# The last layer normalization of a decoder step: weight multiplied in by GpSimd, shift and bias as a rank-six product in PSUM, one pass of VectorE

## The reference

```python
def layer_norm(x, g, b):
    xf = x.astype(F32)
    mu = jnp.mean(xf, -1, keepdims=True)
    var = jnp.mean(jnp.square(xf - mu), -1, keepdims=True)
    return ((xf - mu) * lax.rsqrt(var + LN_EPS) * g.astype(F32) + b.astype(F32)).astype(x.dtype)
...
h = layer_norm(DN_ALPHA * x + mixed, ln1_g, ln1_b)
f, fbuf = conv_ffn(h, ffn_buf, ffn_w_up, ffn_conv_w, ffn_w_down)
y = layer_norm(DN_ALPHA * h + f, ln2_g, ln2_b)
```

## Time and profile before

| | us |
|---|---|
| median of 3 runs | 2952.71 |
| lowest, highest | 2946.45, 2958.77 |
| span of the profiled execution (first to last instruction) | 2947.1 |
| its own time | not given by the page |
| last chunk of the down projection | about 2824 to 2919 |
| tail, behind the last product | about 2919 to 2947.1 |

### The profile page before, as it was taken

One profiled execution on the slowest core, in us unless ns is written; L12 is line 12 of the kernel. 1 busy time (PEld: TensorE's weight loads), 2 busy tenths in 40 slices (PEclk: granted clock), 3 DMA queues, 4 the chain that ended last, 5 costly groups with the idle time before them and its releaser, 6 DMA issues.

```text
span 2947.1 us, 55566 instructions
## 1 busy us (share of the span) xinstructions
PE 2788.9 (95%) x22685; PEld 2676.0 (91%) x22685; DVE 2278.0 (77%) x3537; ACT 1384.8 (47%) x2371; POOL 359.2 (12%) x332
## 2 busy tenths in 40 slices
PE   8999999999989969999889999999999999999996
PEld 8999999988888658889889999999999999999996
DVE  6656877877657777755688888888888888878898
ACT  4434545545646544522264444444444453434344
POOL 0010000013370315223330000000000000000002
PEclk9999999999989989999999999999999999999998
DMA  7564444448722884563344444444343464434343
GB/s 221 179 206 107 117 119 128 113 150 286 275 82 105 343 247 117 148 175 92 90 157 136 119 126 117 137 115 132 111 141 111 137 194 163 153 112 155 114 124 118
DMA packets 521474, 440.14 MB, mean 149 GB/s; under 512 B 36264, under 2 KB 476767, under 8 KB 515147
## 3 DMA queue, kind: packets, MB, share of 16 engines
q1 hardware_dynamic: 456662, 300.70, 35.6%
q0 software_dynamic: 20288, 82.91, 7.6%
q10 hardware_dynamic: 44272, 52.98, 5.3%
HBM read 378.31 MB, written 66.55 MB: 151 GB/s over the span
## 4 chain that ended last, share of the span: by engine, by line
PE 49%; DVE 5%; issue 1%; ACT 1%; POOL 1%; DMA 1%; DVEq 0%; ACTq 0%; POOLq 0%
PE i L3363 42%; PE i L140 7%; DVE f_half L3869 1%; DMA x_blocks<-s_blk 1%; POOL x_blocks L3311 1%; DVE x_blocks L3907 1%; DVE h_rows L3902 0%; DVE y_rows L4000 0%; DVE w_ring L3858 0%; DVE x_blocks L3835 0%; PE i L3372 0%; DVE y_rows L3993 0%; DVE f_sum L3862 0%; DVE ln_parts L3913 0%; ACT x_blocks L3657 0%
## 5 line engine op out<-in xcount | busy, mean ns | idle before, releaser
L3363 PE MATMUL i<-x_blocks,f_half 128*128 128x272 f32 x10752 | 1357.0, 288 | 26.0 <-DVE h_rows L3902 10.9
L3363 PEld LDWEIGHTS i<-x_blocks,f_half 128*128 128x128 f32 x10752 | 1347.0, 189 | 31.7 <-DVE x_blocks L3907 14.1
L570 PE MATMUL a<-xb_in,w_half 128*128 128x272 f32 x4200 | 546.9, 291 | 8.9 <-DVE w_half L972 4.6
L570 PEld LDWEIGHTS a<-xb_in,w_half 128*128 128x128 f32 x4200 | 536.0, 190 | 18.2 <-issue 7.2
L3586 ACT CAST f_half<-w_ring 128x1024 fp32r<-128x1024 f32 (+2 forms) x370 | 346.2, 936 | 403.1 <-PE i L3363 339.5
L3869 DVE TENSOR_TENSOR f_half<-w_ring,f_half 128x1024 fp32r<-128x1024 f32 (+2 forms) x362 | 393.4, 1087 | 80.3 <-ACT f_half L3586 77.9
L3869 DVE TENSOR_TENSOR f_half<-f_sum,f_half 128x1024 fp32r<-128x1024 f32 (+2 forms) x148 | 159.5, 1078 | 81.4 <-ACT f_half L3586 81.4
L972 DVE TENSOR_TENSOR w_half<-w_ring,w_half 128x1024 fp32r<-128x1024 f32 x129 | 157.5, 1222 | 82.9 <-ACT w_half L708 82.5
L3586 ACT CAST f_half<-f_sum 128x1024 fp32r<-128x1024 f32 (+2 forms) x148 | 138.8, 938 | 150.1 <-PE i L3363 148.9
L3323 POOL TENSOR_TENSOR f_half<-w_ring,f_half 128x512 fp32r<-128x512 f32 x8 | 12.9, 1611 | 1397.0 <-ACT f_half L3586 1397.0
L708 ACT CAST w_half<-w_ring 128x1024 fp32r<-128x1024 f32 x125 | 131.3, 1050 | 108.9 <-PE a L570 104.8
(11 more groups left out here) (576 smaller groups left out, 4170.3 us busy)
## 6 DMA issues: line engine op xcount, KB each, us to landing
w_ring<-in_ffn_w_up_dram SPq DMA_DIRECT2D x88, 1024.0 KB, 6.9
w_ring<-in_w_in_dram SPq DMA_DIRECT2D x52, 1024.0 KB, 8.8
w_ring<-in_ffn_w_down_dram SPq DMA_DIRECT2D x24, 1536.0 KB, 7.9
w_ring<-in_w_o_dram SPq DMA_DIRECT2D x16, 1024.0 KB, 6.1
x_blocks<-s_blk ACTq DMA_DIRECT2D x17, 816.0 KB, 5.9
s_proj<-st ACTq DMA_DIRECT2D x48, 272.0 KB, 2.7
s_blk<-x_sums ACTq DMA_DIRECT2D x22, 544.0 KB, 6.7
kv_ring<-in_cmp_w_dram SPq DMA_DIRECT2D x16, 512.0 KB, 8.1
```

The source lines that it names most:

```text
L570: last = nc.tensor.matmul(ps[bank][:, 0:HT2], half(q, w)[:, k], XB[v[j]][:, k], start=j in (0, 1, 3) and k == 0 and i == 0, stop=k == HK - ...
L3363: last = nc.tensor.matmul(ps[bank][:, 0:HT2], half(e, j, wl_)[:, s], XB[:, x0 + s, xl_, BLK_OF[j]], start=start and s == 0 and i == 0, sto ...
```

## The change

The formula is rearranged. With s = -mean * rstd, y_out = (y * g) * rstd + (s * g + b).

- y * g: seven multiplications of 128 x (4 x 256) elements on GpSimd (`times_g`), one for each two blocks whose statistics have been taken, in pairs 2 to 7 of the last chunk, behind GpSimd's subtraction of the pair, and one behind the last pair; the last two blocks are multiplied on VectorE, 128x512 each, in the tail.
- s * g + b: a product with six rows, [1, s_high, 1, s_high, 0, s_low] by [b_high, g_high, b_low, g_low, b_high, g_high]. The rows of g and b are split by GpSimd in pair 6 (a copy and a subtraction of 2x2048 elements), and copied to their partitions by two DMAs of SP. The columns with s are made by VectorE in the tail, turned by four transposes into bank 6, and copied to SBUF by ScalarE. Then 16 products of 128x512 go through banks 0 to 5.
- VectorE does one pass, y * rstd + PSUM, 16 pieces of 128x512. All prompt tiles are done by it, and eight stores of 512 KB are issued by SP. ScalarE and GpSimd keep the two halves of the sample rows, starting behind ScalarE's copy of the turned shift.
- The broadcast loads of weight and bias (2 MB) move from the end of SP's queue to the place behind `down_load(27)`, four pairs earlier; two loads of 8 KB follow behind `down_load(29)`.
- The last block is turned into banks 0 and 1, without waiting for the copy of the one before it; in the last pair two `parts` move one step ahead. The copies of weight and bias into PSUM are gone, and the five tiles are aggregated together.

```diff
             GROW, BROW = GRB[:, 0], GRB[:, 1]
+            BG_RAW = at("ln2_bg_raw", [2, DM], F32, h_at)
+            BG_LO = at("ln2_bg_lo", [2, DM], F32R, h_at)
+            BG = at("ln2_bg", [6, DM], F32R, h_at + 4 * row)
+            SH_T = at("ln2_shift_t", [P, QT, 6], F32, s_at + 224)
+            SH_HI = at("ln2_shift_hi", [P, QT], F32R, s_at + 320)
+            SH = at("ln2_shift_rows", [6, QT * P], F32R, x_at + 3 * KT * P * 4 + 1920)
...
+            P_XG = KT - 2
+
+            def turn_bank(m):
+                return 6 if m < KT - 1 else 0
...
+                    if g == 3 * HK + 3:
+                        sp.wait_ge(xq, 28)
+                        sp.wait_ge(tout, 32 * (FT // 4))
+                        sp.dma_start(GROW, A["ln2_g"].partition_broadcast(P)[:, 0, :]).then_inc(gr_in, 16)
+                        sp.dma_start(BROW, A["ln2_b"].partition_broadcast(P)[:, 0, :]).then_inc(gr_in, 16)
+                    if g == 3 * HK + 5:
+                        sp.wait_ge(tr, 6)
+                        sp.dma_start(BG_RAW[0:1], A["ln2_b"]).then_inc(bg_in, 16)
+                        sp.dma_start(BG_RAW[1:2], A["ln2_g"]).then_inc(bg_in, 16)
...
+                sp.wait_ge(bg_lo, BL0 + 1)
+                sp.dma_start(BG[2:4, :].bitcast(F32), BG_LO[:, :].bitcast(F32)).then_inc(bg_rows, 16)
+                sp.dma_start(BG[4:6, :].bitcast(F32), BG[0:2, :].bitcast(F32)).then_inc(bg_rows, 16)
+                for t in range(QT):
+                    for h in range(2):
+                        sp.wait_ge(yr, 4 * t + 2 * h + 2)
+                        sp.dma_start(O[0][0, t * P:(t + 1) * P, half_cols(h)], YN[:, t, half_cols(h)]).then_inc(y_out, 16)
+                sp.wait_ge(y_out, 16 * 2 * QT)
+                sp.wait_ge(yp_out, YO0 + 32)
...
+                def times_g(m):
+                    cols = slice(m * P, (m + 2) * P)
+                    gp.wait_ge(bst, m + 2)
+                    g = GROW[:, cols].rearrange("p (o n) -> p o n", o=1).broadcast_to((P, QT, 2 * P))
+                    nc.gpsimd.tensor_tensor(YN[:, 0:QT, cols], YN[:, 0:QT, cols], g, ALU.mult).then_inc(xg, 1)
...
+                    i = e - NU - 3 * HK
+                    if i == 2:
+                        gp.wait_ge(gr_in, 32)
+                    if i >= 2:
+                        times_g(2 * (i - 2))
+                    if i == 6:
+                        gp.wait_ge(bg_in, BI0 + 32)
+                        gp.wait_ge(tr, 10)
+                        nc.gpsimd.tensor_copy(BG[0:2, :], BG_RAW[:, :]).then_inc(bg_hi, 1)
+                        gp.wait_ge(bg_hi, BH0 + 1)
+                        nc.gpsimd.tensor_tensor(BG_LO[:, :], BG_RAW[:, :], BG[0:2, :].bitcast(F32), ALU.subtract).then_inc(bg_lo, 1)
+                times_g(KT - 4)
+                for h in range(2):
+                    cols = half_cols(h)
+                    y = YN[0:NS, QT, cols]
+                    gp.wait_ge(nz, NZ0 + h + 1)
+                    nc.gpsimd.tensor_tensor(y, y, GROW[0:NS, cols], ALU.mult).then_inc(yp, 1)
+                    gp.wait_ge(yp, YP0 + 2 * h + 1)
+                    nc.gpsimd.tensor_tensor(y, y, BROW[0:NS, cols], ALU.add).then_inc(yp, 1)
+                    gp.wait_ge(yp, YP0 + 2 * h + 2)
...
-                    if m:
+                    if m and m < KT - 1:
                         pe.wait_ge(cp, m)
+                    b = turn_bank(m)
                     for tt in range(QT):
-                        nc.tensor.transpose(ps[6][:, tt * P:(tt + 1) * P], ht(m)[:, tt * P:(tt + 1) * P], ident)
-                    nc.tensor.transpose(ps[7][0:NS, 0:P], ht(m)[:, SEQ:TOK], ident).then_inc(tr, 1)
+                        nc.tensor.transpose(ps[b][:, tt * P:(tt + 1) * P], ht(m)[:, tt * P:(tt + 1) * P], ident)
+                    nc.tensor.transpose(ps[b + 1][0:NS, 0:P], ht(m)[:, SEQ:TOK], ident).then_inc(tr, 1)
...
+                pe.wait_ge(cp, KT - 1)
+                pe.wait_ge(sh, SH0 + 1)
+                for t in range(QT):
+                    last = nc.tensor.transpose(ps[6][0:6, t * P:(t + 1) * P], SH_T[:, t, :], ident)
+                last.then_inc(sh_t, 1)
+                pe.wait_ge(cp, KT)
+                pe.wait_ge(bg_rows, BR0 + 32)
+                pe.wait_ge(sh_r, SR0 + 1)
+                for u in range(4 * QT):
+                    t, q = u // 4, u % 4
+                    if u >= 6:
+                        pe.wait_ge(yr, u - 5)
+                    nc.tensor.matmul(ps[u % 6][:, :], SH[:, t * P:(t + 1) * P], BG[:, q * Q4:(q + 1) * Q4], start=True, stop=True).then_inc(cs, 1)
...
-                act.wait_ge(ed, 7 * 4 * HK)
-                act.wait_ge(gr_in, 32)
-                for q in range(4):
-                    nc.scalar.copy(ps[q][:, :], GROW[:, q * Q4:(q + 1) * Q4]).then_inc(gp_s, 1)
                 act.wait_ge(bst, KT + 1)
-                nc.scalar.activation(RD[:, QT - 1:], MV[:, QT - 1:, 1], ACT.Sqrt, bias=EPS[:, 0:1]).then_inc(dev, 1)
-                act.wait_ge(bst, KT + 2)
-                nc.scalar.activation(RD[:, 0:QT - 1], MV[:, 0:QT - 1, 1], ACT.Sqrt, bias=EPS[:, 0:1]).then_inc(dev, 1)
+                nc.scalar.activation(RD[:], MV[:, :, 1], ACT.Sqrt, bias=EPS[:, 0:1]).then_inc(dev, 1)
+                act.wait_ge(sh_t, ST0 + 1)
+                nc.scalar.copy(SH[:, :], ps[6][0:6, :]).then_inc(sh_r, 1)
                 act.wait_ge(nm, NM0 + 1)
-                for k, (t, h) in enumerate(P_UNITS):
-                    r = P if t < QT else NS
-                    y = YN[0:r, t, half_cols(h)]
-                    nc.scalar.activation(y, y, ACT.Identity, scale=RD[0:r, t:t + 1], bias=NMR[0:r, t:t + 1]).then_inc(nz, 1)
-                    if k == 0:
-                        for q in range(4):
-                            nc.scalar.copy(ps[4 + q][:, :], BROW[:, q * Q4:(q + 1) * Q4]).then_inc(gp_s, 1)
+                for h in range(2):
+                    y = YN[0:NS, QT, half_cols(h)]
+                    nc.scalar.activation(y, y, ACT.Identity, scale=RD[0:NS, QT:], bias=NMR[0:NS, QT:]).then_inc(nz, 1)
 
             @block.vector
             def _(dve):
...
-                        if c == 3 and i and n == 6:
+                        if c == 3 and i and n == (6 if more else 5):
                             parts(2 * (i - 1))
+                        if not more and n == 6:
+                            parts(KT - 3)
                 add_down(NP - 1, 6)
-                for m in range(KT - 3, KT):
+                for m in range(KT - 2, KT):
                     parts(m)
                 dve.wait_ge(bst, KT)
-                for first, to in ((QT - 1, QT + 1), (0, QT - 1)):
-                    for tt in range(first, to):
-                        r = P if tt < QT else NS
-                        last = nc.vector.bn_aggr(MV[0:r, tt], BS[0:r, tt])
-                    last.then_inc(bst, 1)
+                for tt in range(QT + 1):
+                    r = P if tt < QT else NS
+                    last = nc.vector.bn_aggr(MV[0:r, tt], BS[0:r, tt])
+                last.then_inc(bst, 1)
+
+                def times_g(m):
+                    cols = slice(m * P, (m + 1) * P)
+                    g = GROW[:, cols].rearrange("p (o n) -> p o n", o=1).broadcast_to((P, QT, P))
+                    nc.vector.tensor_tensor(YN[:, 0:QT, cols], YN[:, 0:QT, cols], g, ALU.mult).then_inc(xg, 1)
+
+                dve.wait_ge(gr_in, 32)
+                times_g(P_XG)
                 dve.wait_ge(dev, 2)
-                link.link(nc.vector.reciprocal(RD[:, QT - 1:], RD[:, QT - 1:]))
-                nc.vector.scalar_tensor_tensor(NMR[:, QT - 1:], MV[:, QT - 1:, 0], -1.0, RD[:, QT - 1:], ALU.mult, ALU.mult).then_inc(nm, 1)
-                dve.wait_ge(dev, 3)
-                link.link(nc.vector.reciprocal(RD[:, 0:QT - 1], RD[:, 0:QT - 1]))
-                dve.wait_ge(gp_s, GP0 + 4)
-                base = link.n
-                n = 0
-                for group in V_GROUPS:
-                    for t, q in group:
-                        y = YN[:, t, q * Q4:(q + 1) * Q4]
-                        nc.vector.scalar_tensor_tensor(y, y, MV[:, t, 0:1], ps[q][:, :], ALU.subtract, ALU.mult).then_inc(lk1, 1)
-                    for t, q in group:
-                        y = YN[:, t, q * Q4:(q + 1) * Q4]
-                        n += 1
-                        dve.wait_ge(lk1, base + n)
-                        if t == 0:
-                            dve.wait_ge(gp_s, GP0 + 5 + q)
-                        nc.vector.scalar_tensor_tensor(y, y, RD[:, t:t + 1], ps[4 + q][:, :], ALU.mult, ALU.add).then_inc(yr, 1)
+                link.link(nc.vector.reciprocal(RD[:], RD[:]))
+                nc.vector.scalar_tensor_tensor(NMR[:], MV[:, :, 0], -1.0, RD[:], ALU.mult, ALU.mult).then_inc(nm, 1)
+                dve.wait_ge(nm, NM0 + 1)
+                link.link(nc.vector.tensor_copy(SH_HI[:], NMR[:, 0:QT]))
+                nc.vector.tensor_tensor(SH_T[:, :, 5], NMR[:, 0:QT], SH_HI[:].bitcast(F32), ALU.subtract)
```

(9 more changed lines are left out.)

41 lines of the change are left out of this document (9 added, 32 removed).

## The result

The kernel after takes 2961.45 us (median of 7 runs, 2953.69 to 2966.01), the kernel before 2952.66 (median of 7, 2946.45 to 2958.77): ratio 1.003, interval 1.0018 to 1.0042. So it is slower by 5 to 12 us, 8.8 by the medians. The prediction was 2960.3 us (2946 to 2967), with "within 0.5%" as the likeliest outcome. The size and its direction hold.

A forecast was written before the change was run, and what follows sets the result against it. VectorE was taken to set the pace in the last chunk's pairs, with about 1.0 us of slack, and in the tail. Span 2947.1 - 4.4 (tail) + 12.05 (pairs) = 2954.8 us; median 2952.71 + 7.6 = 2960.3 us, range 2946 to 2967.

The forecast's parts named there:

- Pairs 3 to 5: Last chunk of the down projection: VectorE's subtraction waits 2.07 us for GpSimd's multiplication, 0.85 us reach TensorE in each pair.
- Pair 2: Last chunk: the multiplication waits for the weight rows, starts near 2855.4 just ahead of another VectorE subtraction, costing 1.2 us.
- Pair 6: Last chunk: multiplication, 2x2048 copy and subtraction delay VectorE's first sum for the next pair; cost 7.9 us (5 to 10).
- Pair 7: Last pair of the last chunk: VectorE has less to do, so the multiplication costs 0.4 us.
- Pairs 0 and 1: First two pairs of the last chunk: no term in the sum of what the pairs lose.
- The tail: Behind the last product: gives back about 4.4 us (2.5 to 5.5).
- Steps 1 to 5: Tail: aggregation 0.6 us earlier, weight multiplication, shift, transposes, copy, first product, then sixteen VectorE additions of 10.5 us to 2938.9.
- steps 6 and 7: Tail's two ends: VectorE's rows at 2941.9, queue costing 0 to 0.7 us; GpSimd's sample rows later, at 2942.8.
- The signs: Trace of after: longer pairs, VectorE subtractions and sum delayed behind GpSimd, a long TensorE wait, GpSimd's store ending the tail.
- A: Rival, chance 0.2: GpSimd's multiplications in the pairs are hidden and no pair gets longer; 2948.3 us.
- B: Rival, chance 0.15: slack absorbs nothing, the copy costs as much as the subtraction; pairs lose 20.5 us, 2968.8 us.
- C: Rival, chance 0.05: the tail doesn't get shorter, through its longer chain or full store queue; 2964.8 us.

The follow-up runs named there:

- neither: The kernel after with the edits of small_split and no_mult together, weight missing in 14 of 16 blocks: 2949.73 us, ratio 0.9993 to before.
- memset_mult: The kernel after with each GpSimd multiplication replaced by three memsets of about the same total length: 2957.89 us, ratio 1.0014 to before.
- no_mult: The kernel after without GpSimd's seven multiplications, the 2x2048 copy and subtraction staying in pair 6: 2956.48 us, ratio 1.0007 to before.
- small_split: The kernel after with weight and bias split on 128 partitions, in pair 4, and brought to rows through HBM: 2953.74 us, ratio 1.0005 to before.
- less_stores: The kernel after with two of eight 512 KB prompt stores left out: 2956.2 us, one execution.
- less_stores_early: early_sample with two of eight 512 KB prompt stores left out: 2962.27 us, one execution.
- windows: small_split with GpSimd's multiplications cut to 128x512 and moved to where VectorE has no two-SBUF-input work: 2952.07 us, ratio 0.9999 to before.
- early_sample: The kernel after with ScalarE normalizing the first half of the sample rows before copying the turned shift: 2961.87 us, ratio 1.0031 to before.

## Why the prediction was right or wrong

The total lies 1.2 us from the forecast. It had the pairs 0.6 us too dear and the tail 1.3 us too cheap. That the sum is so near is partly luck: in pair 6 two errors of about 1 us cancel.

**Pairs 3 to 5** (0.85 each forecast, 0.62 measured over neither). The mechanism is shown: taking the reads away takes the loss away (memset_mult). The order was wrong. I put GpSimd ahead since it is issued first; in the trace VectorE had the turn at 2897.94, and the subtraction one later paid. It met only the rest of the multiplication and waited 1.5 us instead of 2.07; the slack took 0.9. The three pairs together differ from the forecast by 0.7 us. The Trainium skill (SBUF — State Buffer, "SBUF: two separate sides") calls the shared port an exclusive lock for the whole instruction. The trace agrees with the whole instruction (the VectorE operation ends 0.54 us behind GpSimd's), and who is served first is not what the order of issue says.

**Pair 2** (1.2 forecast, 0.96 measured): held. The multiplication waits for the weight rows and starts 5.56 us behind the marker (2855.4 - 2849.9 = 5.5 forecast), and here GpSimd has the first turn:

```profile
2864.17 2.43 POOL L3337 TENSOR_TENSOR y_rows<-y_rows,ln_gb 128x1024 f32<-128x1024 f32 x1 [4.69 <-DMA ln_gb<-in_ln_b_dram]
...
2864.71 2.45 DVE L3906 TENSOR_TENSOR f_half<-w_ring,f_half 128x512 fp32r<-128x512 f32 x1
```

**Pair 6** (7.9 forecast, 7.38 measured): held in each sign, the sum of 4.87 us and TensorE's wait of 5.88. The copy took 2.35 us in after, with the wait for its turn, and 1.89 in no_mult, for 2.9 in the sum. The estimate of 1.7 us that came from the Trainium skill's line rate (GPSIMD Engine Reference, Engine selection) was the nearer one to the 1.89; the scaled 256-element copy was too dear (eight times the length took 4.9 times its 0.388 us). GpSimd's three instructions end 10.33 us behind the multiplication's issue (2910.31 to 2920.64), where the prediction has 2909.7 - 2898.76 = 10.9 (its terms add up to 11.1).

What follows their end is right in size for the wrong reason. The prediction let VectorE's first sum wait for the last subtraction, with 7.8 us of work behind it. In the trace the second sum does (L3891), so there was 1 us less to do: 0.56 us to its end and then the 6.24 that small_split shows, 6.8 us. The prediction also held that TensorE's products would "still be ahead of VectorE" at a lower clock. They were not, and that cost 1.0 us. Together they make the 7.83 us from 2920.64 to the marker.

**Pair 7** (0.4 forecast, 1.28 measured). Mis-sized. Here GpSimd did have the first turn. Timeline of after:

```profile
2930.06 2.39 POOL L3337 TENSOR_TENSOR y_rows<-y_rows,ln_gb 128x1024 f32<-128x1024 f32 x1
2930.27 2.72 DVE L3906 TENSOR_TENSOR f_half<-w_ring,f_half 128x512 fp32r<-128x512 f32 x1 [0.21 <-ACT f_half L3628]
```

The multiplication comes 1.59 us behind the marker there instead of 1.13, since GpSimd's own subtraction was also late. VectorE's subtraction is late as well, since TensorE, behind from the lower clock, releases the cast before it late. In small_split, where pair 6 doesn't disturb it, pair 7 costs nothing; in memset_mult it costs 0.73 us though nothing of GpSimd's reads beside it. So it is an echo of pair 6 and not a term of its own.

**Pairs 0 and 1** were at nothing in the sum. There the profile shows GpSimd's own low half, work of before too, taking the turn first and a long VectorE subtraction of `x_blocks` behind it:

```profile
2830.87 1.68 POOL L3343 TENSOR_TENSOR f_half<-w_ring,f_half 128x512 fp32r<-128x512 f32 x1 [1324.32 <-ACT f_half L3628]
2831.34 2.35 DVE L3944 TENSOR_TENSOR x_blocks<-x_blocks 128x1088 fp32r<-128x1088 f32 x1
```

In before it was the other way round (1.29 us for that subtraction). From the `x_blocks` subtraction ahead of it to the marker, before takes 28.7 us (from 2821.17) and after 30.0 (from 2828.59): 1.3 us that the table doesn't hold. In less_stores the same turn is taken (2.35 us again), in less_stores_early it is not (1.28), though up to there the code is one. Five of the eleven traces of new kernels have that turn, and the same stretch takes 28.4 (windows) to 30.5 us (memset_mult). So I count this as spread; whether the change makes that turn likelier was not tried, and one trace of before can't tell.

**The tail** (-4.4 forecast, -3.1 measured). Steps 1 to 5 and the issue of 7 each hold within some 0.3 us: aggregation 0.67 earlier (0.6), the short steps 0.9 (0.8), four transposes 1.01 (1.15), copy 0.57 (0.59), first product 1.03 (0.7), sixteen additions 10.62 (10.5). The mis-sized term is what follows the last issues, in steps 6 and 7. The 3.0 us of before were carried over to both, with "0 to 0.7" for the queue in step 6, and 0 in the sum. 4.9 us were measured behind the last addition and 4.55 behind GpSimd's last DMA; the latter is the one that the sum goes by, 1.55 us too short, and the DMA went out 0.3 earlier than forecast. The prediction had both numbers at hand, 400 GB/s asked for and 418 at best, and read them as "neither gains nor loses much". With two stores less, 1.0 us comes back. That GpSimd's end is the later one held by name in after, but not as a cause: 2.2 us off it left the end where it was (early_sample).

**The signs.** Pairs 3 to 5 took 12.55 to 12.57 us (12.8 forecast), the VectorE subtraction 2.20 (2 to 3), the sum in pair 6 4.87 (about 5), TensorE's wait 5.88 (over 5), and the end came 25.5 us behind the last product (about 24).

**The rivals.** A is out for pairs 2 to 6: none of them with a multiplication stays at 11.95. Only in the last pair, and undisturbed by pair 6, is one hidden (small_split 12.37, neither 12.38). B is out in its sum (pairs +11.5, it decides at 19.2), but its copy was dearer than the truth and its order of turns is what pair 7 shows. C had the right direction for the tail: its store queue is real, but of the 4.4 us only 1.3 are missing, and 1.0 comes back when stores are left out.

## What to carry to other kernels

Before work is given to an idle GpSimd, look at what VectorE does at that moment: beside a GpSimd operation that reads SBUF, VectorE's operations with two SBUF inputs waited for its end here, and the price was what of that wait VectorE's slack (0.9 to 1.2 us in a pair) didn't take, not GpSimd's time. So keep such an operation short (a row on 128 partitions instead of 2), place it beside VectorE's PSUM work, and expect two of them in one place to cost more than their sum (11.5 us here instead of 7.6): the slack is there once, and a TensorE that has stood still may come back at the lower clock. Where a tail ends in stores that already use the queue to some 95% (400 of 418 GB/s), a faster engine ahead of them is only partly worth its gain.

## What the runs showed of the hardware that was not expected

- The instruction issued first doesn't always have the first turn, and the lead doesn't decide it. GpSimd led by 0.19 us at 2897.75 in after and came second; it led by 0.03 (windows, 2866.14), 0.21 and 0.54 us (after, 2930.06 and 2864.17) and came first. With the same lead of 0.47 us at the same place in the code it was first in after (2830.87) and second in windows:

```profile
2828.87 2.90 POOL L3360 TENSOR_TENSOR f_half<-w_ring,f_half 128x512 fp32r<-128x512 f32 x1 [1324.82 <-ACT f_half L3650]
2829.34 1.28 DVE L3966 TENSOR_TENSOR x_blocks<-x_blocks 128x1088 fp32r<-128x1088 f32 x1
```

- A copy with one input on GpSimd takes the turn as well: beside the 2.35 us CAST of 2x2048 a VectorE sum took 2.19 us instead of 0.69. A memset does not.
- Two rows of 2048 cost GpSimd 4.82 us to subtract, the same numbers as 128x32 0.76.
- A store of 128 KB on GpSimd's queue lands in 3.9 us beside stores of 512 KB every 1.33 us, in 3.1 with two of these left out.
